# The first block of a hybrid GLA and short-conv layer: products from the unnormalised input, the reciprocal root mean square applied to their results

## The reference

```python
n = _rmsnorm(h, norm_w[i])                 # x * rsqrt(mean(x*x) + EPS) * w, per token
z = n @ w_in[i]
q, k, v, g_gla, a_low, cb, cc, cu, g_conv = jnp.split(z, idx, axis=-1)
log_a = jax.nn.log_sigmoid((a_low @ w_alpha_up[i] + b_alpha[i])) / GATE_TAU
o_gla = _gla_chunked(qh, kh, vh, log_a)    # state per chunk of 64 tokens, 4 heads
y_gla = _rmsnorm(o_gla, gla_norm_w[i]) * silu(g_gla)
y_conv = cb * _causal_depthwise_conv(cc * cu, conv_w[i], conv_b[i]) * silu(g_conv)
h = h + concat([y_gla, y_conv]) @ w_out[i]
h = h + sigmoid(h @ w_ple_gate[i] + b_ple_gate[i]) * (p[i] @ w_ple[i])
return _rmsnorm(h, final_norm_w)
```

## Time and profile before

| | us |
|---|---|
| median of 3 runs (2111.0 to 2117.63) | 2116.06 |
| the profiled execution | 2112.37 |
| its span | 2110.6 |
| PE busy | 2035.0 (96%) |
| DVE busy | 1366.8 (65%) |
| ACT busy | 733.7 (35%) |
| POOL busy | 597.9 (28%) |

### The profile page before, as it was taken

The page is one execution under the profiler, slowest core; times in us unless marked ns, Lnnn a source line. Parts: engine busy times, 40 slices in busy tenths (PEclk is TensorE's granted clock), DMA queues, the critical chain, the costliest instruction groups (busy, mean ns, idle before and its releaser), DMA issues.

```text
span 2110.6 us, 25958 instructions
## 1 busy us (share of the span) xinstructions
PE 2035.0 (96%) x9762; PEld 1679.3 (80%) x9762; DVE 1366.8 (65%) x1537; ACT 733.7 (35%) x1062; POOL 597.9 (28%) x610
## 2 busy tenths in 40 slices
PE   4999999999999999999999999999999999999997
PEld 3777877787878788888888888888887888888885
DVE  7678778778676476756755765764565355555553
ACT  3444434444344333233333323323223233333331
POOL 7756667566655311111121121121211000000000
PEclk9999999999999999999999999999999999999998
DMA  6353453544545751223621125563376522222221
GB/s 216 119 201 150 160 191 133 189 163 156 198 144 195 312 195 36 95 81 144 259 85 56 60 85 217 207 234 131 115 249 238 181 90 90 90 80 74 78 76 40
DMA packets 82487, 306.71 MB, mean 145 GB/s; under 512 B 10192, under 2 KB 18784, under 8 KB 71904
## 3 DMA queue, kind: packets, MB, share of 16 engines
q1 hardware_dynamic: 53088, 179.14, 23.3%
q0 software_dynamic: 29312, 126.40, 16.7%
HBM read 183.87 MB, written 121.63 MB: 145 GB/s over the span
## 4 chain that ended last, share of the span: by engine, by line
PE 63%; POOL 16%; DMA 12%; issue 5%; DVE 2%; ACT 0%; SPq 0%; POOLq 0%; DVEq 0%; ACTq 0%
PE bank L990 14%; PE bank L992 14%; PE bank L996 14%; PE bank L757 6%; PE bank L758 6%; PE bank L765 5%; POOL PB L617 4%; DMA w_scratch<-prep_hi 4%; POOL PB L604 3%; POOL prep_hi L612 3%; DMA PB<-w_gate_dram 2%; POOL w_scratch L616 2%; DMA PB<-w_in_dram 2%; PE bank L1078 1%; PE bank L1076 1%
## 5 line engine op out<-in xcount | busy, mean ns | idle before, releaser
L990 PE MATMUL bank<-XH,WC 128*128 128x512 f32 x1344 | 526.4, 392 | 2.4 <-DVE xt L1763 2.3
L992 PE MATMUL bank<-XH,WC 128*128 128x512 f32 x1344 | 524.6, 390 | 0.0
L996 PE MATMUL bank<-XL,WC 128*128 128x512 f32 x1344 | 524.3, 390 | 0.0
L1597 DVE TENSOR_TENSOR XL<-RQ,XH 128x1024 fp32r<-128x1024 f32 x168 | 203.7, 1247 | 236.2 <-ACT XH L1292 235.0
L990 PEld LDWEIGHTS bank<-XH,WC 128*128 128x128 f32 x1344 | 253.3, 188 | 56.2 <-DVE xt L1763 2.7
L996 PEld LDWEIGHTS bank<-XL,WC 128*128 128x128 f32 x1344 | 253.2, 188 | 52.8
L992 PEld LDWEIGHTS bank<-XH,WC 128*128 128x128 f32 x1344 | 253.3, 188 | 52.1
L702 POOL TENSOR_TENSOR RQ<-RQ 128x1024 f32<-128x1024 f32 x48 | 115.7, 2433 | 485.5 <-DVE RQ L1616 469.3
L1292 ACT ACTIVATE XH<-RQ 128x1024 fp32r<-128x1024 f32 x168 | 170.7, 1053 | 170.7 <-PE bank L996 155.9
L758 PE MATMUL bank<-XH,WG 128*128 128x512 f32 x512 | 199.3, 389 | 0.0
L757 PE MATMUL bank<-XH,WG 128*128 128x512 f32 x512 | 199.3, 389 | 0.0
(11 more groups left out here) (184 smaller groups left out, 3513.7 us busy)
## 6 DMA issues: line engine op xcount, KB each, us to landing
WC<-w_scratch SPq DMA_DIRECT2D x21, 2048.0 KB, 8.9
RQ<-n_scratch POOLq DMA_DIRECT2D x32, 1024.0 KB, 5.4
w_scratch<-prep_hi POOLq DMA_DIRECT2D x84, 256.0 KB, 2.4
w_scratch<-PB POOLq DMA_DIRECT2D x84, 256.0 KB, 2.3
raw<-xb_dram SPq DMA_DIRECT2D x32, 512.0 KB, 6.6
n_scratch<-raw SPq DMA_DIRECT2D x8, 2048.0 KB, 6.5
y_scratch<-y_sb SPq DMA_DIRECT2D x64, 256.0 KB, 2.5
RQ<-y_scratch POOLq DMA_DIRECT2D x16, 1024.0 KB, 5.6
```

The lines of the kernel that those rows point to most:

```text
L990: nc.tensor.matmul(bank[:], WC[:, i, q, 0, k], xh, start=(k == 0 and i in (P1, P2, P5)), stop=False, skip_group_check=True)
L992: nc.tensor.matmul(bank[:], WC[:, i, q, 1, k], xh, start=False, stop=False, skip_group_check=True)
L996: mm = nc.tensor.matmul(bank[:], WC[:, i, q, 0, k], xl, start=False, stop=(k == 3), skip_group_check=True)
L1597: nc.vector.tensor_tensor(XL[:, k], RQ[:, OPERAND[s % 7], 2 * h:2 * h + 2], XH[:, k].bitcast(F32), ALU.subtract).then_inc(sx_lo, 1)
```

## The change

For block 0 alone, `XH` is made by ACT from `raw` times the norm weight (a scale per partition), with no root mean square in it, slice by slice between the squares, and `XL` by DVE as `raw * weight - XH`, between the sums. The weight vector `vec` gets a semaphore of its own and is loaded right behind `raw`. All 14 products of the block are made from these, and the reciprocal root mean square goes to the results: for k and v, whose rows are tokens, as a scale per partition in ACT's copy out of PSUM (`tok`, four columns that PE makes with four small matmuls); for q (`scale_q`) and g (`scale_g`), whose columns are tokens, as a multiplication by `R_first` on DVE. g is therefore copied first and its Silu taken in block 1 (`first_silus`). Block 0 is still normalised for `n_scratch`, later, on DVE. POOL makes no `XL` any more. ACT's squares and DVE's sums for block 1 are moved behind block 0's log-sigmoid.

```diff
 (SP)
             load_raw(raw, xb[0], 0)
+            sp.dma_start(vec[:], vectors).then_inc(vec_loaded, 16)
...
-            sp.dma_start(vec[:], vectors).then_inc(consts_loaded, 16)
...
-            sp.wait_ge(first_n, 8)
             store_n(0)
 (POOL)
                 if n == W_V:
-                    lo_of_block_0(HALF_A, first_hi, first_lo)
                     pool.wait_ge(w_ready, 2)
...
-                if n == W_V + 1:
-                    lo_of_block_0(HALF_B, x_hi, x_lo)
 (PE)
-                    if ahead:
-                        pe.wait_ge(first_hi, k + 1)
-                    elif first:
+                    if early and k % 2 == 0:
+                        pe.wait_ge(w_ready, k // 2 + 1)
+                    if first:
                         pe.wait_ge(x_hi, 8 * step + k + 1)
...
             def x_stats(s):
                 if is_first(s):
                     pe.wait_ge(x_sum, 7)
+                    for t in range(TT):
+                        mm = nc.tensor.matmul(ps[O_BANK[0]][:, t:t + 1], R[:, t * P:t * P + P],
+                                              ones[:, 0:1].bitcast(F32), start=True, stop=True)
+                    mm.then_inc(tok_mean, 1)
                     mean_of(SMALL, R[:]).then_inc(x_mean, 1)
...
                 ka_tile(b, 1)
                 if tail:
                     head_stat(b - 1, 0)
+                else:
+                    x_stats(0)
                 ka_tile(b, 2)
...
-            pe.wait_ge(consts_loaded, 80)
-            x_stats(0)
+            pe.wait_ge(consts_loaded, 64)
             pe.wait_ge(suffix_ready, 1)
 (ACT)
+            def scale_of(b, t):
+                if not is_first(b):
+                    return 1.0
+                act.wait_ge(tok_rstd, 1)
+                return tok[:, t:t + 1]
...
-                evacuate(b, t, ka_sb[:, t], ps[MAIN[t % 3]][:, 0:KA])
+                evacuate(b, t, ka_sb[:, t], ps[MAIN[t % 3]][:, 0:KA], scale=scale_of(b, t))
...
-                evacuate(b, 10 + h, sg[:, h], ps[MAIN[(10 + h) % 3]][:], ACT.Silu)
+                evacuate(b, 10 + h, sg[:, h], ps[MAIN[(10 + h) % 3]][:], ACT.Copy if is_first(b) else ACT.Silu)
+            def first_silus():
+                for h in range(HEADS):
+                    act.wait_ge(first_g, h + 1)
+                    nc.scalar.activation(sg[:, h], sg[:, h], ACT.Silu).then_inc(first_silu, 1)
...
-            x_squares(0, range(KT))
-            x_rms(0)
-            act.wait_ge(consts_loaded, 80)
+            act.wait_ge(vec_loaded, 16)
+            for k in range(KT):
+                if k % 2 == 0:
+                    act.wait_ge(raw_loaded[k // 2], 16)
+                nc.scalar.activation(XH[:, k], raw[:, k], ACT.Copy,
+                                     scale=vec[:, V_NORM + k:V_NORM + k + 1]).then_inc(x_hi, 1)
+                x_squares(0, (k,))
+            act.wait_ge(consts_loaded, 64)
             nc.scalar.activation(suffix[:], mask[:, 0:P], ACT.Copy).then_inc(suffix_ready, 1)
-            for k in range(KT):
-                act.wait_ge(first_n, k + 1)
-                nc.scalar.activation(XH[:, k, HALF_A], raw[:, k, HALF_A], ACT.Copy).then_inc(first_hi, 1)
...
+            act.wait_ge(tok_mean, 1)
+            nc.scalar.activation(tok[:], ps[O_BANK[0]][:, 0:TT], ACT.Sqrt, bias=eps[:], scale=1.0 / D_MODEL).then_inc(
+                tok_root, 1)
+            x_rms(0)
 (DVE)
+            def scale_q(t):
+                dve.wait_ge(evacuated, 9 + t)
+                for odd in range(2):
+                    rows = slice(DK * odd, DK * odd + DK)
+                    q = q_diag[t][rows, :, odd]
+                    nc.vector.tensor_tensor(q, q, R_first[rows, :].rearrange("p (c t) -> p c t", c=NCH),
+                                            ALU.mult).then_inc(first_q, 1)
+            def scale_g(h):
+                dve.wait_ge(evacuated, 11 + h)
+                nc.vector.tensor_tensor(sg[:, h], sg[:, h], R_first[:], ALU.mult).then_inc(first_g, 1)
...
-            x_sums(0, range(1, KT))
-            dve.wait_ge(consts_loaded, 80)
-            dve.wait_ge(x_root, 1)
-            for half, rstd, n_done, hi_done, lo_done in ((HALF_A, first_rstd, first_n, first_hi, first_lo),
-                                                         (HALF_B, x_rstd, n_ready, x_hi, x_lo)):
...
+            dve.wait_ge(vec_loaded, 16)
+            for k in range(KT):
+                dve.wait_ge(x_hi, k + 1)
+                nc.vector.scalar_tensor_tensor(out=XL[:, k], in0=raw[:, k], scalar=vec[:, V_NORM + k:V_NORM + k + 1],
+                                               in1=XH[:, k].bitcast(F32), op0=ALU.mult, op1=ALU.subtract).then_inc(
+                    x_lo, 1)
+                if k > 0:
+                    x_sums(0, (k,))
...
+            dve.wait_ge(tok_root, 1)
+            nc.vector.reciprocal(tok[:], tok[:]).then_inc(tok_rstd, 1)
+            dve.wait_ge(x_root, 1)
+            dve.wait_ge(v_lo, V_BY_DVE)
+            nc.vector.reciprocal(R_first[:], R[:]).then_inc(x_rstd, 1)
+            dve.wait_ge(x_rstd, 1)
+            normalise(0, range(KT), R_first)
             over_blocks(dve, gla, apart=2)
```

More of the change, by code:

```diff
@@ L36 @@
 EPS = 1e-6
-FIRST_LO = 3
 V_BY_DVE = 2
-HALF_A, HALF_B = slice(0, TB // 2), slice(TB // 2, TB)
 BIG = D_MODEL * 4
@@ L119, in build @@
         gamma = sb("gamma", [P, 2, NCH])
+        tok = sb("tok", [P, TT])
         suffix = over("suffix", [P, P], mask_at, F32R)
@@ L171, in build @@
         rt = over("rt", [P, TB], sg_at + 5 * ROW)
+        R_first = over("R_first", [P, TB], sg_at + 5 * ROW)
         sum_hi = over("sum_hi", [P, TB], sg_at + 6 * ROW, F32R)
@@ L748, in big_tile @@
                 last = i == TILES[phase] - 1
-                ahead = phase == GLA and is_first(b) and i == 0
-                first = i == (1 if phase == GATE else 2 if phase == GLA and is_first(b) else 0)
+                first = i == (1 if phase == GATE else 0)
+                early = phase == GLA and is_first(b) and i == 0
                 for k in range(KT):
                     hh, lh, hl = products(k)
-                    if ahead:
-                        pe.wait_ge(first_hi, k + 1)
-                    elif first:
+                    if early and k % 2 == 0:
+                        pe.wait_ge(w_ready, k // 2 + 1)
+                    if first:
                         pe.wait_ge(x_hi, 8 * step + k + 1)
@@ L758, in big_tile @@
                     nc.tensor.matmul(acc_ap, lh[0], lh[1], start=False, stop=False)
-                    if ahead:
-                        pe.wait_ge(first_lo, k + 1)
-                    elif first:
+                    if first:
                         pe.wait_ge(x_lo, 8 * step + k + 1)
@@ L811, in ka_tile @@
             def ka_tile(b, t, after=None):
-                if is_first(b):
+                if is_first(b) and t > 0:
                     pe.wait_ge(w_ready, W_V)
@@ L1224, in gla @@
                     head_squares(b - 1, 0)
+                if isinstance(b, int) and b == 1:
+                    first_silus()
                 ka_out(b, 0)
@@ L1234, in gla @@
                 a_out(b)
-                if nxt:
+                if nxt and tail:
                     x_squares(b + 1, range(4))
@@ L1250, in gla @@
                 log_sigmoid_ln(b)
+                if is_first(b):
+                    x_squares(b + 1, range(KT))
                 if tail:
@@ L1416, in _ @@
                     v_hi, 1)
-            for k in range(KT):
-                act.wait_ge(n_ready, k + 1)
-                nc.scalar.activation(XH[:, k, HALF_B], raw[:, k, HALF_B], ACT.Copy).then_inc(x_hi, 1)
+            act.wait_ge(tok_mean, 1)
+            nc.scalar.activation(tok[:], ps[O_BANK[0]][:, 0:TT], ACT.Sqrt, bias=eps[:], scale=1.0 / D_MODEL).then_inc(
+                tok_root, 1)
+            x_rms(0)
             over_blocks(act, gla, apart=2)
@@ L1562, in gla @@
                 log_decay(b)
+                if is_first(b):
+                    x_sums(b + 1, range(1, KT))
                 split_decay(b, 0)
```

42 lines of the change are left out of this document (19 added, 23 removed).

## The result

The changed kernel takes 2134.18 us (median of seven runs, 2124.16 to 2139.51) against 2116.06 of the kernel before on the same chip; the ratio is 1.0076, 95% interval 1.0059 to 1.0093. It is **slower**, by 0.8%, and outside the range of the prediction. Each kernel has one profiled execution, and what is read from a trace belongs to that one. For the changed kernel it took 2136.18 us with a span of 2134.4, against 2112.37 and 2110.6: 23.8 us more, of which the following accounts.

A forecast was written before the change was run, and what follows sets the result against it. POOL's weight preparation was taken to set the end, leading by 4.3 us where PE meets it. PE's −7.3 + 6.1 + 2.8 made it 1.6 us late, the meeting −3.5 us: 2112.5 us against 2116.06, range 2105 to 2120.

The forecast's parts named there:

- The start: Block 0 up to the v tiles: PE's first product at 28.5, v tiles at 44.0 against 51.30, 7.3 us ahead.
- The normalisations: Block 0's eight on DVE before the first logits' bias: end at 53.5; PE wants the result at 56.7.
- third rival: Block 0's normalisations hold DVE's queue to 66, PE waits 9.5 us for the first logits: 2124 us; chance 0.1.
- The added wait for `R_lo`: Block 1's statistics, in the second q tile: PE comes at 77.0, `R_lo` at 82.9; wait 6.1 us, bounds 2.5 and 9.
- The slow clock: PE's next 14 statistics and products after the `R_lo` wait run at a slow clock, adding 2.8 us.
- 1.6 us later than before: When PE leaves block 1's statistics in block 0: −7.3 + 6.1 + 2.8 us.
- The rest of block 0: DVE's added q and g multiplications, 5.5 us, costed at nothing; states late by up to 2 us; Silus nothing to 1.
- The blocks behind: The other 640 us of POOL's way to the end of GLA: effect not readable, no new work.
- POOL's lead: POOL's `QG` work ends at 61.8, 3.3 us ahead; 2.0 after turns with the q and g multiplications.
- second rival: POOL's lead vanishes as its preparation waits for DMAs; only part of the slow clock is won: 2116 us; chance 0.2.
- The meeting: End of GLA: PE arrives at 731.1, `hsq_lo` at 731.8; PE goes on 2.0 us earlier, −3.5 with slow clock won.

The follow-up runs named there:

- e3: Changed kernel with seven of block 0's eight normalisations left out; 2130.87 us, ratio 1.0073.
- e4: Changed kernel with the last two of block 0's normalisations put behind the first bias; 2124.89 us, ratio 1.0043.
- e1: Kernel before, with 54 extra TensorE products ahead of the last g tile of block 0; 2136.38 us, ratio 1.0107.
- e5: Changed kernel, last two normalisations behind the first bias, n stored and raw loaded in quarters, squares and sums partly ahead of the logarithm; 2117.05 us, ratio 1.0008.
- e7: Changed kernel with most of POOL's additions and subtractions for later weights cut from 512 columns to 16; 2095.72 us, ratio 0.9913.
- e8: Changed kernel with POOL held before its second pair's loads, and each even pair until its block's third v tile; 2128.51 us, ratio 1.0063.
- e11: Kernel of e5 with only POOL's even pairs held until their block's third v tile; 2117.38 us, ratio 0.9999.

## Why the prediction was wrong

**The start** was right: `vec` landed at 10.83 (10.7), VectorE's operations took 1.1 to 2.8 us beside POOL, TensorE began at 28.39 (28.5) and the v tiles at 44.06 (44.0), POOL's first `QG` came at 32.05 (32) and its last ended at 60.4 (61.8). That TensorE's start fits to 0.1 us is in part luck. The fifth sum ended at 27.32 (27.5), but POOL's splits had ended at 20.6 (22.4), and VectorE's next four operations took 6.2 us (5.0): the two "beside POOL's DMA issues", at 1.4 us together, were not free, one alone took 2.25.

**The normalisations** failed in size. "With each behind one of POOL's subtractions every second time they end at 53.5": they ended at 60.93, 2.39 us each, each one behind an operation of POOL's. TensorE waited 4.7 us at the logits, where the sum had nothing. That is the third rival, between its two values (0 and 9.5); it had a chance of 0.1, on a row of 1.63 us behind a short POOL operation, though the subtractions of `QG` that stand here take twice as long. The argument against it, "POOL issues DMAs between its operations, in which DVE runs", is what failed: a normalisation that started beside a DMA issue still ended behind POOL's next operation (the row at 47.12), so all eight met one.

**The added wait for `R_lo`** was the right mechanism: 8.3 us against 6.1 (its terms as written, from 77.0 to 82.9, add up to 5.9), the Ln to `R_lo` taking 16.2 us for my 14.0. e3 and e4 show that it is the same chain in both; the gain before it was paid back there in e3, and by half in e4. I had called the store and load of block 1 what the rival would make late; the store took 8.7 us for 7.0, and it did not bind: ScalarE had no wait for `raw` at 76.1.

**The slow clock** was 5.1 us in block 0 for 2.8. With the two sizes above, "1.6 us later than before" became 11.7.

**The rest of block 0** was right within its bound: 0.9 us of wait for `hist`, for a forecast of up to 2.

**The blocks behind** are the step that failed most: "What the other 640 us make of that I can't read; they hold no new work." I carried a difference at the start of block 1 unchanged to the convolutions. e1 shows 11.4 us becoming 32.7 there (753.4 for 720.7), in unchanged work. A sign of it stood in the trace of the kernel before: the loads at the same 38 to 40 us in five blocks out of six, and block 5, where they slip to 44.6 and the wait is 4.6 for 1.7. What an earlier place costs, which is what happened, that trace doesn't show.

**POOL's lead**, 3.3 us and then 2.0 in the forecast, was 4.7 at its first pair and lost by the second. So the second rival's mechanism, a lead that vanishes at POOL's DMAs, came about as well, and POOL's last preparation, forecast 2.0 us sooner than before, ended 9.9 us later. It cost nothing at the end, as TensorE was later still.

**The meeting** was right in kind: TensorE goes on without the 4.31 us of the earlier trace rows. But the forecast counted 5.1 there (from +1.6 to −3.5), and 8.9 came back: 4.4 of waits and 4.5 of slow clock (926.65 busy for 922.10). From the first convolution product to the end it is 1380 to 1382 us where POOL is early (the changed kernel, e1, e3, e5, e7) and 1390 in the kernel before. So the view that the end belongs to the later of the two engines held, but TensorE did not come 1.6 us late; it came 32.6 late.

By the prediction's own arithmetic, the measured 11.7 us of block 0 would have given 11.7 − 4.3 − 2.8 = +4.6, near 2121 us. The other 19 of the profiled execution's 23.8 lie in blocks 1 to 6, less what more came back at the meeting, and no rival had them.

## What to carry to other kernels

Where two engines run loops of nearly commensurate periods and share a resource (here 44 and 88 us), a delay of one is not a number to be carried along: look up where the idle gap of the one lies against the other's critical operation, and ask what the change does to that place. Price an operation that takes turns with another engine by the partner that stands beside it in its new place, and don't take the partner's DMA issues for free time. And a statistic that is moved behind a table function costs its whole chain, from the last table to the engine that waits, however early its data land.

## What was not expected of the hardware

- VectorE's normalisation of 128 x 512 took 2.39 us on the mean beside POOL's long operations, three times its 0.75 alone.
- An operation can lose its turn to one that starts later: in e8 a remainder of 0.68 us starts at 344.85, beside a DMA issue of POOL (344.68 to 345.27), POOL's subtraction at 345.29, and the remainder ends behind it, after 2.27 us. In the kernel before, up to 700 us, 41 of VectorE's sums, remainders and products of 128 x 512 with two inputs in SBUF started beside a DMA issue with POOL's next operation right behind it: 32 of them ended behind that one. Of 18 that started beside a DMA issue with nothing behind it for 2 us, each took 0.68 to 0.75. And in the 11 cases where POOL was idle at VectorE's start and began within 0.6 us of it, VectorE went first. So it is not the issue that costs, but the operation right behind it; why that goes first is open.
- The place has a sharp edge on one side: with the loads 39.9 us into a block the wait is 1.7, with 44.6 mostly 4.6 to 5.1. The place counts against the operation and not the block's start: in block 1 of e8 to e11 TensorE comes to the fourth head 42 to 44 us into the block, for 37 in their later blocks with long waits, and the wait is 1.8 though the loads go at 43 to 45.
- Why the early place, once taken, settles at 19 to 23 us into the block rather than sliding through was not settled by these runs.
